# Three places for split weights instead of two, one of them in the fourth weight room, and the experts' gather copies shared out anew

## The chip, the cores and the metric

One core of one Trainium2 chip runs the whole program. The time is device microseconds of that core. TensorE (PE) multiplies, VectorE (DVE) and ScalarE (ACT) work on what lies in on-chip memory, GpSimd (POOL) does a little, and SyncE (SP) issues nearly all DMA transfers, in the order of its program.

## The reference

A sequence of 256 tokens, 2048 features, goes through two networks, all in float32:

- A first block: RMS norm, a projection to 5120 features (`w_in`), causal pooling and an HGRN2 recurrence, a projection back (`w_out`); cross attention to 256 memory rows (`wk`, `wq`, `wv`, `wo`, each 2048 x 2048); then a hierarchical mixture of experts with 16 experts of 512 features, each token going to 2 of them in one group of 4; then a norm.
- A second block, two layers: `mod = silu(c) @ w_ada + b_ada` (2048 x 6144 for each layer) gives shift, scale and gate; a norm with them, a projection to 6656 features (`w_in_2`, stages z0 and z1 here), four mixers (a 2-D Fourier transform with the matrix `w_fft`, neighbourhood attention, retention in both directions, a convolution of 31 taps with a pointwise matrix), and a projection back (`w_out_2`, stages mix0 and mix1).

## The kernel before

**Blocks.** All large weights come as blocks of 128 x 2048 float32, 1 MB each. The stages are w_in (40 blocks), w_out, wk, wq, wv, wo (16 each), the experts (192), z0 (52), mix0 (16), z1 (52), mix1 (16). Activations lie transposed, features on partitions, 256 tokens along the row.

**Split products.** A float32 product is made of three fp16 products. ScalarE scales a block by 256 and rounds it to fp16, the high half (`split` in its program, the instruction on L644). VectorE subtracts that from the scaled block, which gives the low half (L1292). TensorE then does high x high, low x high and high x low for each of 8 chunks and two halves of a block: 48 matmuls of 256 columns (`product`, L2241). Activations are split in the same way.

**Rooms and places.** A block passes two kinds of buffers. It lands in a room: `raw` has four, and the experts' stage has up to four more in memory that is free then (W, two in Y, one in Z). `raw_rooms` goes through all blocks in the order of loading and gives each the open room that was used longest ago. The small matrices pool_w, w_fft (`fft0`, `fft1`) and the pointwise one (`pw0`, `pw1`) take rooms too, without being split, and hold them until their own matmuls are done (L2818, L2839). From the room the halves are written to a place: `w_hi` and `w_lo` have two (SPL = 2), used in turn. In the experts' stage the same two places, taken together, are one half of a ring of four blocks, and W holds the other half.

**Who waits for whom.** SP loads a block when the room's last block has been split (`raw_taken`, counted by VectorE's low half, or by TensorE for a small matrix; L471). ScalarE splits a block when it has landed and when TensorE has finished the block that had the place (`block_done`). VectorE follows ScalarE (`hi_done`), and TensorE waits for VectorE (`raw_taken`). Each engine runs its program in order.

**The modulation.** The product with w_ada is done on VectorE, in 192 steps spread over the dense stages by a table (`ada_plan`): 16 loads of 512 KB for each of 12 parts, each followed by one multiply-add of 128 x 1024 into a running sum (`ada_step`, L1263, the first of a part L1260). They alternate between two buffers; a load waits until the step two before it has used its buffer (`ada_used`, L476). On VectorE the steps planned for block m come after the split of block m. On SP their loads come after the load of block m + 2 (`load_due(2)`), in the same queue. The table gives z0 and z1 thirteen steps over blocks 2 to 10 (two and one in turn) and one step a block from 11 to 29; wq and wv have 26 steps in 16 blocks, wo 20, mix0 16 over blocks 2 to 11, w_in 16 over 2 to 12, w_out 11, wk 13.

**The other work of VectorE** between splits in z0 and z1: four or so taps of the convolution after each block (L2008), the softmax parts of the attention, and in z0 the first network's last norm.

**The small matrices of z0 and z1.** w_fft is loaded behind block 43, and TensorE uses it just before block 45 (`fft_map`). The pointwise matrix is loaded behind block 48, and used just before block 47.

**The start of the experts.** The rows of the 256 tokens are gathered by group into 448 slots, in 16 chunks, by TensorE (L2556, a product with a matrix of zeros and ones, one for the high and one for the low halves). ScalarE copies the high part of each chunk out of its bank (L976, `gather_hi`), VectorE the low part (L1867, `gather_lo`). TensorE puts the gather of chunk b + 2 into block b and needs the copies of chunk b for block b; two chunks have banks at a time. VectorE has, between the same blocks, the second half of the rows' split (`rows_lo`) and the routing's small operations (`groups_left`, `best_two`, `combine`, `place_rows`).

The lines that matter in `raw_rooms` and in SP's program:

```
        open_ = list(range(RAW))
        if 0 <= j < n:
            open_ += [4] * (j >= 6) + [5] * (7 <= j < 126) + [6] * (j >= 7) + [7] * (13 <= j < 150)
        r = min(open_, key=lambda r: last[r])
```

```
                        load(ph, m, w[2 * n + j % 2, j // 2] if k == 0 and ph in K_MAJOR else w[2 * n + j // 2, j % 2])
                        due.append((ph, plan.get(ph, {}).get(m, [])))
                        load_due(2)
```

Of the kernel before, what the change touches and what calls it, by code (L numbers as in the profile page):

```python
# [8 lines left out]
F16 = mybir.dt.float16  # L9
# [14 lines left out]
ROOMS = RAW + 4  # L24
SPL = 2
IN_ORDER = [4, 5, 2, 3, 6, 7, 0, 1, 8, 9]
# [98 lines left out]
def raw_rooms():  # L125

    (first, _, n), total = places()["moe"], sum(n for _, n, _ in STREAM)
    rooms, uses, last = [], [0] * ROOMS, [-1] * ROOMS
    for b in range(total):
        j = b - first  # L130
        open_ = list(range(RAW))
        if 0 <= j < n:
            open_ += [4] * (j >= 6) + [5] * (7 <= j < 126) + [6] * (j >= 7) + [7] * (13 <= j < 150)
        r = min(open_, key=lambda r: last[r])
        uses[r], last[r] = uses[r] + 1, b
        rooms.append((r, uses[r]))
    return rooms
# [59 lines left out]
def build(nc, A, table, const_at, columns, router, out):  # L197
    ctx = ExitStack()
    with ctx:
# [20 lines left out]
        raw = sb("raw", [P, RAW, BLK])  # L220
        w_hi = sb("w_hi", [P, SPL, BLK], F16)
        w_lo = sb("w_lo", [P, SPL, BLK], F16)
        XT = sb("XT", [P, KC, T])
# [28 lines left out]
        y_hi, y_lo = (Zf[:, k * 1024:(k + 1) * 1024].bitcast(F16).rearrange("p (k n) -> p k n", n=512) for k in range(2))  # L252
        hid_at = [H[:, k * 1024:(k + 1) * 1024] for k in range(4)] + [Zf[:, c * T:c * T + 1024] for c in (28, 48)] + [Yf[:, k * 1024:(k + 1) * 1024] for k in range(2)]
        raw_at = [raw[:, r, :] for r in range(RAW)] + [w3, Yf[:, 0:BLK], Yf[:, BLK:2 * BLK], Zf[:, 40 * T:48 * T]]
        hid_t = [a[:, 0:2 * ROWS_SORTED].bitcast(F16).rearrange("p (c n) -> p c n", n=ROWS_SORTED) for a in hid_at]
# [41 lines left out]
        HI_AT = {"ga": 0, "pt": KC, "t": KC + 3, "y": KC + 3 + 4 * TILES}  # L297
        LO_AT = {"ga": 0, "weight": KC, "t": KC + 1, "y": KC + 1 + 4 * TILES}
        SQ_AT = {"x": 0, "wo": 4, "two": 12, "mix0": 18, "mix1": 26}
# [119 lines left out]

        def done(eng, ph, j, i=0):  # L420

            s = where(ph, j)[1]
            eng.wait_ge(block_done[s % SPL], s // SPL + 1 + 2 * i)

# [30 lines left out]
        def _(sp):  # L455
# [5 lines left out]
            def load(ph, j, src):  # L461
                r, n = rooms[where(ph, j)[0]]
                if n > 1:
                    sp.wait_ge(raw_taken[r], n - 1)
                elif r == 4:
                    sp.wait_ge(ada_mod, 7)
                elif r in (5, 6):
                    done(sp, "wo", 15)
                elif r == 7:
                    sp.wait_ge(S("rows_lo"), 10)  # L470
                sp.dma_start(raw_at[r], src).then_inc(raw_full[r], 16)  # L471
# [149 lines left out]
        def _(act):  # L621
            def split_half(ph, j, half):

                b, s = where(ph, j)
                r, n = rooms[b]
                if half == 0:
                    act.wait_ge(raw_full[r], 16 * n)
                    act.wait_ge(block_done[s % SPL], s // SPL)
                cut = slice(half * BLK // 2, half * BLK // 2 + BLK // 2)
                act.activation(w_hi[:, s % SPL, cut], raw_at[r][:, cut], ACT.Copy, scale=W_SCALE).then_inc(hi_done, 1)  # L630

            def split(ph, j, i=0):
                b, s = where(ph, j)
                r, n = rooms[b]
                act.wait_ge(raw_full[r], 16 * n)
                if ph == "moe":
                    act.wait_ge(block_done[s % SPL], s // SPL - 1)
                    if j < 2:
                        act.wait_ge(S("x_o"), 2 * X_HEADS)
                    w = ring_hi[j // 2 % 2][:, j % 2 * BLK:j % 2 * BLK + BLK]  # L640
                else:
                    act.wait_ge(block_done[s % SPL], s // SPL + 2 * i)
                    w = w_hi[:, s % SPL, :]
                act.activation(w, raw_at[r], ACT.Copy, scale=W_SCALE).then_inc(hi_done, 1)  # L644
                if (ph, j) in parts_due:
                    ada_high(parts_due[ph, j])
# [327 lines left out]
            def gather_hi(c):  # L974
                act.wait_ge(S("moe_mm"), MM_AT["ga"] + c + 1)
                act.activation(xs_hi[:, c, :], gather_bank(c, 0), ACT.Copy).then_inc(S("moe_hi"), 1)  # L976

# [35 lines left out]
            for n in range(MOE_STEPS):  # L1013
                f, last = n // 8, n % 8 == 7
                for part in range(2):
# [16 lines left out]
                    if n >= 17 and n % 16 == 1 and n < GATE_UP + 3:  # L1032
                        for k in (2 * part, 2 * part + 1):
                            turned_hi(n // 16 - 1, k)
                    if n == 2 and part == 1:
                        act.wait_ge(S("r_exp_in"), 1)
# [204 lines left out]
        def _(dve):  # L1241
# [34 lines left out]
            def split_half(ph, j, half):  # L1276

                b, s = where(ph, j)
                dve.wait_ge(hi_done, s + 1 + half)
                cut = slice(half * BLK // 2, half * BLK // 2 + BLK // 2)  # L1280
                ins = dve.scalar_tensor_tensor(w_lo[:, s % SPL, cut], raw_at[rooms[b][0]][:, cut], W_SCALE, w_hi[:, s % SPL, cut], ALU.mult, ALU.subtract)
                if half:
                    ins.then_inc(raw_taken[rooms[b][0]], 1)

            def split(ph, j, i=0):
                b, s = where(ph, j)
                dve.wait_ge(hi_done, s + 1 + 4 * i + (s > at["z1"][1]))
                hi, lo = w_hi[:, s % SPL, :], w_lo[:, s % SPL, :]
                if ph == "moe":
# [575 lines left out]
            def gather_lo(c):  # L1865
                dve.wait_ge(S("moe_mm"), MM_AT["ga"] + c + 1)
                dve.tensor_copy(xs_lo[:, c, :], gather_bank(c, 1)).then_inc(S("moe_lo"), 1)  # L1867

# [31 lines left out]
            for n in range(MOE_STEPS):  # L1900
                f, last = n // 8, n % 8 == 7
                for part in range(2):
# [23 lines left out]
                    if part == 1:  # L1926
                        if n == 0:
                            groups_left()
                        if n == 2:
                            best_two()  # L1930
                        if n == 5:
                            combine()
                        if n in (3, 4):
                            place_rows(n - 3)
                    if n == 6 and part == 1:
# [285 lines left out]
        def _(pe):  # L2221
            def product(ph, j, b, k0, start, stop, groups=None, x=(xh, xl), rows=False, between=None):

                s = at[ph][1] + j
                hi = w_hi[:, s % SPL, :].rearrange("p (c n) -> p c n", c=8)
                lo = w_lo[:, s % SPL, :].rearrange("p (c n) -> p c n", c=8)
                first = start
# [316 lines left out]
            def gather(c):  # L2544
                if c >= 2:
                    pe.wait_ge(S("moe_hi"), HI_AT["ga"] + c - 1)
                    pe.wait_ge(S("moe_lo"), LO_AT["ga"] + c - 1)
                if c == 2:
# [10 lines left out]
            def turn_places():  # L2559
                pe.wait_ge(S("moe_hi"), HI_AT["ga"] + KC)  # L2560
                pe.wait_ge(S("moe_lo"), LO_AT["ga"] + KC)
                pe.wait_ge(S("placed"), 4)
# [80 lines left out]
            for n in range(MOE_STEPS):  # L2643
# [8 lines left out]
                for c in range(2):  # L2652
                    taken(pe, "moe", 2 * n + c)
                    if f == 0:
                        pe.wait_ge(S("moe_hi"), HI_AT["ga"] + 2 * n + c + 1)
                        pe.wait_ge(S("moe_lo"), LO_AT["ga"] + 2 * n + c + 1)
                    if f == 8 and kh % 2 == 0 and c == 0:
# [336 lines left out]
```

## Time and profile before

| | |
|---|---|
| median of 3 runs | 2095.44 us (2094.69 to 2101.43) |
| the profiled execution's own time | 2093.71 us |
| its span | 2091.7 us |
| granted TensorE clock, mean | 0.994 |
| TensorE matmul busy | 2041.4 us (98%) |
| VectorE busy | 1752.3 us (84%) |
| ScalarE busy | 1194.1 us (57%) |
| DMA, mean over the span | 284 GB/s |

The profiled execution's time holds 2 us beside the span, from the first to the last instruction. "Busy" of TensorE is the union of its matmuls, whose ends are modelled: they start every 0.11 us and are shown 0.27 us long, so a gap in the rows is some 0.16 us shorter than what was lost. In the rows, PE, DVE and ACT are TensorE, VectorE and ScalarE, and SPq is SyncE's queue of DMA issues. L1292 is line 1292 of the kernel. A row such as `w_lo<-raw,w_hi` gives output and inputs by their names in the program. `[0.63 <-DVE w_lo L1292]` says that the engine stood idle for 0.63 us before the instruction, and what ended that.

### The profile page before, as it was taken

To read this page: it belongs to the slowest core of one execution; us is meant where nothing else is said; L and a number is where in the kernel's file an instruction comes from. 1 tells how busy PE (TensorE), PEld (TensorE's weight loads), DVE (VectorE), ACT (ScalarE), POOL (GpSimd) and SP (SyncE) were. 2 spreads that over 40 slices of the span, in tenths; PEclk is the share of its full clock that TensorE was granted. 3 is DMA by queue.
4 is the path that set the end of the run, shared out by engine and by line. 5 is a ranking of instruction groups with operands and counts; after the bars stand their busy time and mean duration, and the time that the engine had idled before them with its cause. 6 is when DMAs were issued, how large, how long until landed. Compare 5 with 4: busy or idle time off the path is not lost.

```text
span 2091.7 us, 42599 instructions
## 1 busy us (share of the span) xinstructions
PE 2041.4 (98%) x18993; PEld 1641.1 (78%) x18993; DVE 1752.3 (84%) x1670; ACT 1194.1 (57%) x1071; POOL 41.3 (2%) x40
## 2 busy tenths in 40 slices
PE   8999999999999989999999999999999899999998
PEld 7889888888889946555556568888888788888887
DVE  7875787988888799999999999999668779996555
ACT  5554644444445478877877864456554444565543
POOL 0002300000000000000000000000000000000000
PEclk9999999999999999999999999999999999999999
DMA  8854487789888878999999987874458778744452
GB/s 303 317 202 162 163 314 271 280 307 326 319 326 298 309 280 355 420 420 420 420 420 416 408 318 293 294 256 164 143 184 310 281 286 304 250 162 159 181 202 101
DMA packets 95717, 593.23 MB, mean 284 GB/s; under 512 B 10664, under 2 KB 10824, under 8 KB 36784
## 3 DMA queue, kind: packets, MB, share of 16 engines
q1 hardware_dynamic: 94912, 583.73, 74.4%
q0 software_dynamic: 624, 6.80, 0.8%
q8 instruction: 149, 2.44, 0.5%
q14 instruction: 32, 0.26, 0.0%
HBM read 588.39 MB, written 2.10 MB: 282 GB/s over the span
## 4 chain that ended last, share of the span: by engine, by line
PE 68%; DVE 16%; DMA 10%; ACT 3%; issue 3%; DVEq 0%; SPq 0%; POOL 0%; ACTq 0%; POOLq 0%
PE GB L2241 52%; DVE w_lo L1292 6%; PE GB L2670 4%; DVE W L1292 3%; PE MB L2670 3%; DMA raw<-w_up 3%; DMA W<-w_ada 2%; ACT w_hi L644 2%; DMA Z<-w_ada 2%; DMA raw<-w_down 2%; DVE W L1263 1%; DVE Z L1263 1%; DMA raw<-w_gate 1%; PE MB L2839 1%; PE MB L2441 1%
## 5 line engine op out<-in xcount | busy, mean ns | idle before, releaser
L644 ACT ACTIVATE w_hi<-raw 128x2048 f16<-128x2048 f32 x308 | 588.1, 1910 | 705.5 <-PE GB L2241 680.9
L1292 DVE SCALAR_TENSOR_TENSOR w_lo<-raw,w_hi 128x2048 f16<-128x2048 f32 x308 | 706.0, 2294 | 244.9 <-ACT w_hi L644 244.2
L2241 PE MATMUL GB<-H,w_hi 128*128 128x256 f16 x4352 | 718.9, 273 | 18.3 <-DVE w_lo L1292 11.6
L2241 PE MATMUL GB<-H,w_lo 128*128 128x256 f16 x2176 | 593.8, 273 | 0.0
L2241 PEld LDWEIGHTS GB<-H,w_hi 128*128 128x128 f16 x4352 | 421.6, 98 | 85.0 <-DVE w_lo L1292 16.6
L2241 PEld LDWEIGHTS GB<-H,w_lo 128*128 128x128 f16 x2176 | 213.2, 98 | 24.9
L2241 PE MATMUL GB<-w_hi,H 128*128 128x256 f16 x1280 | 210.7, 273 | 0.0
L1263 DVE SCALAR_TENSOR_TENSOR W<-W,SM 128x1024 f32<-128x1024 f32 x120 | 153.8, 1282 | 31.8 <-DMA W<-w_ada 28.5
L2241 PE MATMUL GB<-w_lo,H 128*128 128x256 f16 x640 | 174.4, 273 | 0.0
L2241 PE MATMUL GB<-Z,w_hi 128*128 128x256 f16 x1024 | 170.0, 274 | 2.9 <-DVE w_lo L1292 2.9
L2241 PE MATMUL GB<-W,w_hi 128*128 128x256 f16 x1024 | 168.0, 273 | 2.7 <-DVE w_lo L1292 2.7
L2241 PE MATMUL GB<-Z,w_lo 128*128 128x256 f16 x512 | 140.4, 274 | 0.0
L2241 PE MATMUL GB<-W,w_lo 128*128 128x256 f16 x512 | 139.6, 273 | 0.0
L2241 PEld LDWEIGHTS GB<-w_hi,H 128*128 128x128 f16 x1280 | 124.7, 98 | 16.1 <-issue 1.3
L1292 DVE SCALAR_TENSOR_TENSOR W<-raw,W 128x2048 f16<-128x2048 f32 x54 | 123.2, 2286 | 2.3 <-ACT W L644 2.2
L644 ACT ACTIVATE W<-raw 128x2048 f16<-128x2048 f32 x54 | 103.0, 1911 | 20.9 <-DMA raw<-w_down 6.1
L2241 PEld LDWEIGHTS GB<-Z,w_hi 128*128 128x128 f16 x1024 | 100.4, 98 | 16.0 <-DVE w_lo L1292 3.8
L2241 PEld LDWEIGHTS GB<-W,w_hi 128*128 128x128 f16 x1024 | 99.9, 98 | 14.9 <-DVE w_lo L1292 3.3
L2008 DVE SCALAR_TENSOR_TENSOR Y<-Y,PC 128x256 f32<-128x256 f32 x240 | 99.6, 479 | 0.0
L2670 PE MATMUL GB<-W,Z 128*64 (+1 forms) x864 | 86.7, 353 | 4.4 <-DVE Z L1867 4.3
L2670 PE MATMUL MB<-W,Z 128*64 (+1 forms) x864 | 86.0, 353 | 1.3 <-DVE W L1292 1.2
L1263 DVE SCALAR_TENSOR_TENSOR Z<-Z,SM 128x1024 f32<-128x1024 f32 x60 | 76.8, 1281 | 10.7 <-DMA Z<-w_ada 9.9
(489 smaller groups left out, 2789.9 us busy)
## 6 DMA issues: line engine op xcount, KB each, us to landing
raw<-w_in SPq DMA_DIRECT2D x144, 1024.0 KB, 5.2
W<-w_ada SPq DMA_DIRECT2D x128, 512.0 KB, 5.6
raw<-w_out SPq DMA_DIRECT2D x48, 1024.0 KB, 5.1
raw<-w_down SPq DMA_DIRECT2D x41, 1024.0 KB, 10.6
raw<-w_gate SPq DMA_DIRECT2D x34, 1024.0 KB, 11.0
raw<-w_up SPq DMA_DIRECT2D x32, 1024.0 KB, 12.8
Z<-w_ada SPq DMA_DIRECT2D x64, 512.0 KB, 5.9
raw<-xattn_wk SPq DMA_DIRECT2D x16, 1024.0 KB, 5.1
```

The source lines that it names most:

```text
L644: act.activation(w, raw_at[r], ACT.Copy, scale=W_SCALE).then_inc(hi_done, 1)
L1263: dve.scalar_tensor_tensor(sums, w, SM[:, 24 + k:25 + k], sums, ALU.mult, ALU.add).then_inc(ada_used[n % 2], 1)
L1292: dve.scalar_tensor_tensor(lo, raw_at[r], W_SCALE, hi, ALU.mult, ALU.subtract).then_inc(raw_taken[r], 1)
L2008: dve.scalar_tensor_tensor(ca[:, c, :], CU[:, c, k // 4:k // 4 + T], col("conv_w_2", l * TAPS * 4 + k), ca[:, c, :], ALU.mult, ALU.add).th ...
L2241: last = pe.matmul(o, a, m, start=first, stop=end and w_part is lo, skip_group_check=True)
L2441: ins = pe.matmul(MB[:, h % 2, a * T:a * T + T], x_q[q][:, 4 * h + c, a * P:a * P + P], x_k[k][:, 4 * h + c, :], start=a == 0 and c == 0 a ...
L2670: ins = pe.matmul(o_bank(j, k)[r:r + SLOT], x[:, c0 + c, at_:at_ + SLOT], v, start=kh == 0 and c == 0 and part == 0, stop=kh == 7 and c == ...
L2839: ins = pe.matmul(banks[:, n // 2, n % 2 * T:n % 2 * T + T], w[:, k, n * P:n * P + P], x[:, k, :], start=n % 2 == 0 and k == 0, stop=k == ...
```

## The change

- SPL is 3. The third place for split weights lies in the fourth room (`raw[:, 3]`, which holds both halves of one block). `slot` turns a block's number into its place. The dense stages use three rooms and three places; the experts' stage has the fourth room back from its fifth block on.
- The first load into that room in the experts' stage waits for block 13 of wo, the last that was split there. The first block of z0 waits until the room is given up.
- In the gather, ScalarE copies both parts of odd chunks, first the low and then the high one; VectorE copies the low part of even chunks alone. LO_AT and the waits of TensorE count accordingly.
- groups_left comes two steps later, best_two one step, the second place_rows two, the first one step; ScalarE's first exponential comes one step later.

```diff
-SPL = 2
+SPL = 3
...
-        open_ = list(range(RAW))
+        open_ = list(range(RAW - 1))
         if 0 <= j < n:
-            open_ += [4] * (j >= 6) + [5] * (7 <= j < 126) + [6] * (j >= 7) + [7] * (13 <= j < 150)
+            open_ += [3] * (j >= 4) + [4] * (j >= 6) + [5] * (7 <= j < 126) + [6] * (j >= 7) + [7] * (13 <= j < 150)
...
+        third = raw[:, RAW - 1, :].bitcast(F16)
+        hi_of = [w_hi[:, 0, :], w_hi[:, 1, :], third[:, 0:BLK]]
+        lo_of = [w_lo[:, 0, :], w_lo[:, 1, :], third[:, BLK:2 * BLK]]
+
+        def slot(s):
+
+            return (s + 2) % SPL
...
                 if n > 1:
                     sp.wait_ge(raw_taken[r], n - 1)
+                elif r == RAW - 1:
+                    done(sp, "wo", 13)
...
                 if ph == "moe":
-                    act.wait_ge(block_done[s % SPL], s // SPL - 1)
+                    act.wait_ge(block_done[(s - 4) % SPL], (s - 4) // SPL + 1)
...
                 else:
-                    act.wait_ge(block_done[s % SPL], s // SPL + 2 * i)
-                    w = w_hi[:, s % SPL, :]
+                    act.wait_ge(block_done[s % SPL], s // SPL)
+                    if (ph, j) == ("z0", 0):
+                        given_up(act, RAW - 1)
+                    w = hi_of[slot(s)]
...
             def gather_hi(c):
                 act.wait_ge(S("moe_mm"), MM_AT["ga"] + c + 1)
+                if c % 2:
+                    act.activation(xs_lo[:, c, :], gather_bank(c, 1), ACT.Copy)
                 act.activation(xs_hi[:, c, :], gather_bank(c, 0), ACT.Copy).then_inc(S("moe_hi"), 1)
...
             def gather_lo(c):
-                dve.wait_ge(S("moe_mm"), MM_AT["ga"] + c + 1)
-                dve.tensor_copy(xs_lo[:, c, :], gather_bank(c, 1)).then_inc(S("moe_lo"), 1)
+                if c % 2 == 0:
+                    dve.wait_ge(S("moe_mm"), MM_AT["ga"] + c + 1)
+                    dve.tensor_copy(xs_lo[:, c, :], gather_bank(c, 1)).then_inc(S("moe_lo"), 1)
...
-                        if n == 0:
+                        if n == 2:
                             groups_left()
-                        if n == 2:
+                        if n == 3:
                             best_two()
                         if n == 5:
                             combine()
-                        if n in (3, 4):
-                            place_rows(n - 3)
+                        if n in (4, 6):
+                            place_rows(n // 2 - 2)
...
-                    pe.wait_ge(S("moe_lo"), LO_AT["ga"] + c - 1)
+                    pe.wait_ge(S("moe_lo"), LO_AT["ga"] + c // 2)
...
-                        pe.wait_ge(S("moe_lo"), LO_AT["ga"] + 2 * n + c + 1)
+                        pe.wait_ge(S("moe_lo"), LO_AT["ga"] + n + 1)
```

## Rows read from the trace of the kernel before

**Rows 1.** Waits of TensorE and VectorE: us in total, times, longest
```profile
PE GB L2241 <- DVE w_lo L1292: 17.3, 20, 2.1
PE GB L2670 <- DVE Z L1867: 5.2, 5, 1.6
...
DVE W L1263 <- DMA W<-w_ada: 28.5, 33, 1.8
DVE Z L1263 <- DMA Z<-w_ada: 9.9, 9, 2.7
```
**Rows 2.** The page's groups: busy us, mean ns | idle before them, releaser
```profile
L644 ACT ACTIVATE w_hi<-raw 128x2048 f16<-128x2048 f32 x308 | 588.1, 1910 | 705.5 <-PE GB L2241 680.9
```
**Rows 3.** Timeline of TensorE in wk and mix0: start us, us, instruction, idle before
```profile
402.03 0.39 PE L2241 MATMUL GB<-H,w_hi 128*128 128x256 f16 x2 [0.63 <-DVE w_lo L1292]
...
1633.61 0.39 PE L2241 MATMUL GB<-W,w_hi 128*128 128x256 f16 x2 [1.49 <-DVE w_lo L1292]
```
**Rows 4.** Timeline of SP's queue in z0: start us, us of the issue
```profile
1321.11 0.33 SPq L471 DMA_DIRECT2D raw<-w_in  x1
1322.31 0.33 SPq L476 DMA_DIRECT2D Z<-w_ada  x1
```
**Rows 5.** Timeline of VectorE in z0, the same stretch
```profile
1318.79 2.29 DVE L1292 SCALAR_TENSOR_TENSOR w_lo<-raw,w_hi 128x2048 f16<-128x2048 f32 x1
1320.99 1.28 DVE L1263 SCALAR_TENSOR_TENSOR Z<-Z,SM 128x1024 f32<-128x1024 f32 x1
1322.19 1.67 DVE L2008 SCALAR_TENSOR_TENSOR Y<-Y,PC 128x256 f32<-128x256 f32 x4
1323.77 2.29 DVE L1292 SCALAR_TENSOR_TENSOR w_lo<-raw,w_hi 128x2048 f16<-128x2048 f32 x1
```
**Rows 6.** w_ada issued behind weights: two from 300.5, two from 331.9, three from 402.4
```profile
DMA to landing us min/median/max: 5.9/6.4/6.8
...
DMA to landing us min/median/max: 5.7/6.5/7.3
...
DMA to landing us min/median/max: 7.0/8.3/8.5
```
**Rows 7.** Windows: span, busy PE, PEld, DVE, ACT, POOL, clock, DMA share, GB/s
```profile
1267.00:1316.00 49.00, 47.51 (x432) 42.11 (x432) 45.97 (x49) 20.52 (x15) 0.00 (x0) 1.00 0.92 350
1316.00:1360.00 44.00, 43.84 (x412) 38.90 (x413) 43.09 (x55) 19.20 (x14) 0.00 (x0) 1.00 0.84 294
1360.00:1440.00 80.00, 79.43 (x707) 66.82 (x705) 79.52 (x115) 49.51 (x82) 0.00 (x0) 1.00 0.64 221
738.00:775.00 37.00, 33.27 (x280) 15.76 (x282) 34.97 (x46) 28.93 (x29) 0.00 (x0) 1.00 0.79 286
```
**Rows 8.** Chain of waits in wq, from one head's scores to the next's
```profile
496.87 2.62 PE MB L2441 x24
499.49 15.72 PE GB L2241 x144
...
520.89 2.62 PE MB L2441 x24
```
**Rows 9.** SP's wait for w_fft's room, that load's landing, the chain behind
```profile
SPq L471 <- PE GB L2818: 22.9, 1, 22.9
...
DMA to landing us min/median/max: 4.8/4.8/4.8
...
1528.96 10.64 PE GB L2241 x96
1539.60 6.92 PE MB L2839 x32
```
**Rows 10.** A wait of TensorE at the experts' start, and the gather's copies
```profile
754.00 0.84 PE L2670 MATMUL GB<-W,Z 128*64 x6 [1.65 <-DVE Z L1867]
...
L1867 DVE CAST Z<-MB x16: 616/618/625, 735.8 to 789.9; 128x448 f16<-128x448 f32 x16
...
L976 ACT ACTIVATE Z<-MB x16: 521/526/543, 735.8 to 786.9; 128x448 f16<-128x448 f32 x16
```

More of the change, by code:

```diff
@@ L220, in build @@
         raw = sb("raw", [P, RAW, BLK])
-        w_hi = sb("w_hi", [P, SPL, BLK], F16)
-        w_lo = sb("w_lo", [P, SPL, BLK], F16)
+        w_hi = sb("w_hi", [P, 2, BLK], F16)
+        w_lo = sb("w_lo", [P, 2, BLK], F16)
         XT = sb("XT", [P, KC, T])
@@ L297, in build @@
         HI_AT = {"ga": 0, "pt": KC, "t": KC + 3, "y": KC + 3 + 4 * TILES}
-        LO_AT = {"ga": 0, "weight": KC, "t": KC + 1, "y": KC + 1 + 4 * TILES}
+        LO_AT = {"ga": 0, "weight": KC // 2, "t": KC // 2 + 1, "y": KC // 2 + 1 + 4 * TILES}
         SQ_AT = {"x": 0, "wo": 4, "two": 12, "mix0": 18, "mix1": 26}
@@ L418, in piece_end, with done @@
             return 2 + u if i == 0 and ph in K_MAJOR else 4 * i + 2 * u + 1
-        def done(eng, ph, j, i=0):
+        def done(eng, ph, j):
             s = where(ph, j)[1]
-            eng.wait_ge(block_done[s % SPL], s // SPL + 1 + 2 * i)
+            eng.wait_ge(block_done[s % SPL], s // SPL + 1)
         def pieces_in(eng, k):
@@ L629, in split_half @@
                 cut = slice(half * BLK // 2, half * BLK // 2 + BLK // 2)
-                act.activation(w_hi[:, s % SPL, cut], raw_at[r][:, cut], ACT.Copy, scale=W_SCALE).then_inc(hi_done, 1)
+                act.activation(hi_of[slot(s)][:, cut], raw_at[r][:, cut], ACT.Copy, scale=W_SCALE).then_inc(hi_done, 1)
             def split(ph, j, i=0):
@@ L1034, in _ @@
                             turned_hi(n // 16 - 1, k)
-                    if n == 2 and part == 1:
+                    if n == 3 and part == 1:
                         act.wait_ge(S("r_exp_in"), 1)
@@ L1280, in split_half @@
                 cut = slice(half * BLK // 2, half * BLK // 2 + BLK // 2)
-                ins = dve.scalar_tensor_tensor(w_lo[:, s % SPL, cut], raw_at[rooms[b][0]][:, cut], W_SCALE, w_hi[:, s % SPL, cut], ALU.mult, ALU.subtract)
+                ins = dve.scalar_tensor_tensor(lo_of[slot(s)][:, cut], raw_at[rooms[b][0]][:, cut], W_SCALE, hi_of[slot(s)][:, cut], ALU.mult, ALU.subtract)
                 if half:
@@ L1287, in split @@
                 dve.wait_ge(hi_done, s + 1 + 4 * i + (s > at["z1"][1]))
-                hi, lo = w_hi[:, s % SPL, :], w_lo[:, s % SPL, :]
+                hi, lo = hi_of[slot(s)], lo_of[slot(s)]
                 if ph == "moe":
@@ L2224, in product @@
                 s = at[ph][1] + j
-                hi = w_hi[:, s % SPL, :].rearrange("p (c n) -> p c n", c=8)
-                lo = w_lo[:, s % SPL, :].rearrange("p (c n) -> p c n", c=8)
+                hi = hi_of[slot(s)].rearrange("p (c n) -> p c n", c=8)
+                lo = lo_of[slot(s)].rearrange("p (c n) -> p c n", c=8)
                 first = start
@@ L2560, in turn_places @@
                 pe.wait_ge(S("moe_hi"), HI_AT["ga"] + KC)
-                pe.wait_ge(S("moe_lo"), LO_AT["ga"] + KC)
+                pe.wait_ge(S("moe_lo"), LO_AT["ga"] + KC // 2)
                 pe.wait_ge(S("placed"), 4)
```

## The prediction, made before the change was run

> **What bounds the kernel now.** Read the busy table first: TensorE is busy 98% of the span, so at most the rest can come back, and any stall put into it counts in full. Then TensorE's waits [rows 1]: 20 waits in the dense stages for the low half of a weight block (17.3 us), and 5 for VectorE's gather copies (5.2 us). VectorE in turn waits for w_ada, 38 us in 42 waits, in the same group. Third, the split itself [rows 2]: ScalarE makes the high half in 1.91 us and idles 681 us waiting for TensorE to give a place back. With two places the split of a block can't begin before the block two ahead is done; a block is 5.24 us of TensorE (three take 15.72, [rows 8]), and 1.91 + 2.29 us of split leave about 1 us for delays. That is what produces the 20 waits; two are shown [rows 3].
>
> Last, who feeds VectorE. SP's queue is in order: weight load, then the modulation loads (w_ada, 512 KB) of the block two earlier, then the next weight load. A weight load waits for a free room, i.e. for VectorE's split of the block that had it. In [rows 4, 5] the split at 1318.79 ends at 1321.08 and the load goes out at 1321.11; the step at 1320.99 ends at 1322.27 and the next w_ada load goes out at 1322.31. That load is used two blocks on. VectorE's block there is 4.98 us (1318.79 to 1323.77): split 2.20, step 1.20, four taps 1.58 (start to start, as everywhere below), with no DMA wait.
>
> **The rooms.** With three rooms instead of four, the load of block m+2 waits for the split of m-1, not of m-2, and w_ada for block m comes behind it in SP's queue. So w_ada for m cannot be issued before the split of m-1 has ended, plus 0.10 us and the 0.37 us of the weight load's issue, and VectorE wants it about 5 us after that same moment. How long such a load takes, directly behind a weight block, is in [rows 6]: seven of them, 5.7 to 8.5 us. I take 6.4 (the median of the first two groups, whose queue is otherwise empty, as it would be); 5.7 and 7.3 are my ends. The cover that hid it was the second block of distance; it is gone.
>
> This makes a loop of two blocks on VectorE that TensorE has no part in, so that a third place for split weights can't shorten it: end of split m-1, 0.47, landing 6.4, steps of m, work behind them, split of m+1 (2.20).
> - Middle of z0 and z1 (blocks 11 to 19, one step, taps 1.58): 0.47 + 6.4 + 1.20 + 1.58 + 2.20 = 11.85, 5.93 us a block. TensorE needs 5.4 ([rows 7]: 43.8 us busy, eight blocks and their small work). 9 x 0.53 = 4.8 us.
> - Blocks 3 to 10 (every other one has two steps): 0.47 + 6.4 + 2.40 + 2.20 = 11.5, 5.75 us; now 49 us for nine, 5.44 [rows 7]. 8 x 0.31 = 2.5 us.
> - Blocks 20 to 29: VectorE is full there (79.5 of 80 us, [rows 7]; some 6.5 us a block, 3.1 of it behind the step): 0.47 + 6.4 + 1.2 + 3.1 + 2.2 = 13.4, 6.7 us. 10 x 0.2 = 2 us.
>
> That is 9.3 us in each of z0 and z1, 18.6 in all. At 5.7 us it is 1.6 each (3 in all), at 7.3 it is 21 each (42).
>
> The Trainium skill (DMA: Bandwidth & Descriptors, "Anatomy of one DMA") gives a DMA a fixed 2.0 us and its bytes at 436 GB/s, in a fit for the gpsimd path. By it the 1.5 MB of a weight block and a w_ada load behind it would be down 5.6 us after the first issue, so 5.2 after the second. The trace does not agree: its fastest is 5.7 and its median over 6 [rows 6]. By the page the middle blocks would take 5.33 us, and the loop would cost nothing.
>
> The same loop elsewhere:
> - w_in, blocks 2 to 12: 1.5 steps a block, little behind them; 5.65 against 5.24, less idle time that VectorE has at its start: +3 (0 to +7).
> - w_out, wk: steps are sparse and VectorE has slack ahead of the waits, so a place in advance takes up what delays there are: -1.5 (two waits such as [rows 3]'s first, with some 0.16 us of pipeline each). The longest wait of [rows 1], 2.1 us at w_out's start, is one for the order of ScalarE's work and stays. The room of pool_w now goes to w_out's second block; its release at 260.1 still leaves several us before that split. Ends -4 and +3.
> - wq, wv, wo: four blocks take 24.0 us [rows 8], 6.0 each. A two-step block makes the loop 0.47 + 6.4 + 2.4 + 0.9 + 2.2 = 12.4, 6.2 a block; with the one-step blocks between, 6.1 to 6.3. Over 48 blocks 5 to 14 us, of which one place in advance absorbs 5: +4 (0 to +15).
> - mix0: VectorE enters it idle, so the place in advance is full and covers 5.24 us of a lag of about 6.4, where TensorE now waits some 2.7 in all (its last in [rows 3]): -1.5 (-3 to +3).
>
> **The small matrices in z0 and z1.** The w_fft matrix takes a room from its load until its matmuls at block 45. With four rooms the next in that room is block 47; with three it is block 46. SP's wait for it is in [rows 9] (22.9 us, off the path today). After: the load goes out at 1528.8, lands 4.8 us later (1533.6), high half 1.91 + 0.05, low half 2.29: ready at 1537.9. TensorE starts block 45 at 1528.96 and is through it at 1534.2. +3.7 us in each of z0 and z1, +7.4; no split place helps, since the raw data is not there. The pointwise matrix now waits for the split of block 46 (1537.9) and lands about 5 us later, when TensorE is through with that block (1543.1): it adds 0 to 2. Ends +7 and +12 for both.
>
> **The experts' rows.** VectorE drops eight copies of 0.62 us (0.54 apart), ScalarE gains eight of 0.53 (0.45 apart), [rows 10]. VectorE is the full one (35.0 of 37 us against 28.9, the last of [rows 7]). Walked from 741: chunk 3's copy, now behind ScalarE's split of block 4, is ready near 746.8 where block 3 wants it at 748.0: that wait goes. ScalarE's extra copy of chunk 1 delays splits 2 and 3 by 0.45. For block 4 VectorE loses chunk 3's copy (0.54) and groups_left (1.12, moved to step 2), and the copy ends at 752.7 instead of 753.86: the 1.65 wait becomes about 0.5 plus what block 3 starts earlier. Blocks 5 to 8 then start on time, in place of waits of 0.61 and 0.51. Block 8 starts at 765.9 instead of 768.5: -2.6 us. best_two, combine and place_rows only change place (same instructions). The weight loads follow VectorE's splits, so they move with it and the DMA-bound part behind keeps the gain. Ends: -4 (all waits gone) and +1 (ScalarE late, or DMA takes it back).
>
> The waits on the last room before and after the experts (block 13 of wo; the room given up at block 187) are met long before; the first block loads of the experts need one room more to be split, some 25 us ahead of use: 0.
>
> **Sum.** 18.6 + 3 - 1.5 + 4 - 1.5 + 7.4 - 2.6 = +27.4. On the profiled execution's own time, 2093.71 us: 2121. The median of the three runs lies 1.7 above that execution; I keep 2121.
>
> **Rivals.**
> - *The lead wins (faster).* If w_ada behind a weight block lands under 5.35 us (2 x 5.4 less 0.47, 1.20, 1.58 and 2.20), the loop costs nothing; the 14 waits that aren't ones of a stage's start (six, 6.4 us) go (17.3 - 6.4 = 10.9, plus 14 x 0.16), and the experts' 2.6: -15.7; with the w_fft room +7.4, -8.3: 2085, or 2078 if that is covered too. For: VectorE idles hundreds of us behind ScalarE, so slack exists. Against: not in the stretches with steps, where it idles under 1 us per 40. Chance 0.10. The page's reckoning above (the Trainium skill, "Anatomy of one DMA") would put it here.
> - *It cancels (no change).* Landings at the low end (5.7): +3 for z, +1 for w_in, +7.4, and -11 from w_out to wk, mix0 and the experts at their low ends: 2094, 2098 if one of them gives less. Chance 0.08.
> - *The pair of loads is slow (much slower).* With 7.3 us or more, as in [rows 6]'s last group, and in the first part of z0 where the DMA engines are 92% busy [rows 7]: 42 for z, 6 for w_in, 14 for wq to wo, 9 for the small matrices: about 2160. Chance 0.16.
> - *The forecast*: 0.66.
>
> This kernel's measurement tells about 0.3% (6 us) from no change. Faster 0.10, same 0.08, slower 0.82. The likeliest case's own range is 2104 to 2140; for 8 in 10 I take 2094 to 2146, which leaves out most of the faster case and the slow end.
>
> **What would show it.** VectorE's waits for w_ada grow from 38 us to over 80, most in z0 and z1, blocks 4 to 19; SP's weight and w_ada issues stand 0.4 us apart there; TensorE's waits for the low half grow at regular 5.9 us steps. One TensorE wait of 3 to 5 us at block 46 in z0 and z1. The waits for L1867 fall from 5.2 to under 3 us. ScalarE's wait for TensorE falls where no steps are (mix1). It is wrong if w_ada behind a weight block lands under 5.3 us, or if TensorE's waits total less than now.

## The result, and the profile after

The changed kernel takes 2161.61 us (median of 4 runs, 2157.32 to 2178.05) against 2095.07 us: ratio 1.0325, 95% interval 1.0265 to 1.0385. It is slower, as forecast, by 66.5 us where 27.4 were forecast (+25.9 against the 2095.07 median); the time lies above the range (2094 to 2146). The profiled execution is the slowest of the four, 2178.05 us with a span of 2176.2, so its terms add up to 84.5 us, not to 66.5. A trace nearer to the median comes from an experiment below.

The totals first: the page of the changed kernel, its span and TensorE's row, and the first lines of its chain of waits.

```profile
span 2176.2 us, 42599 instructions
...
PE 2069.2 (95%) x18993; PEld 1646.7 (76%) x18993; DVE 1750.2 (80%) x1662; ACT 1197.4 (55%) x1079; POOL 42.5 (2%) x40
...
PE 28%; DMA 23%; issue 23%; DVE 23%; ACT 3%; SPq 1%; POOLq 0%; DVEq 0%; POOL 0%; ACTq 0%
PE GB L2256 17%; DMA W<-w_ada 14%; DVE w_lo L1306 8%; DVE W L1277 4%; PE GB L2685 3%; DVE W L1306 3%; PE MB L2685 3%; DMA Z<-w_ada 3%; DMA raw<-w_up 3%; DVE raw L1306 2%; DMA raw<-w_down 2%; ACT w_hi L656 2%; DMA raw<-w_gate 1%; DVE Z L1277 1%; PE MB L2571 1%
```

The span grew by 84.5 us. TensorE has the same 18993 matmuls, but was busy 27.8 us longer (2041.4 to 2069.2); the other 56.7 us are idle time. Those are two different costs, and the prediction had only the second. Of the 27.8 us, 22.2 are a lower clock (below); much of the rest is waits that the rows show too short, by 0.16 us for each of the 39 waits for low halves that are new (an estimate: 6 us). The waits (us in total, times, longest), which answer to [rows 1]:

```profile
DVE W L1277 <- DMA W<-w_ada: 117.7, 69, 4.6
PE GB L2256 <- DVE w_lo L1306: 52.2, 40, 3.9
DVE Z L1277 <- DMA Z<-w_ada: 39.3, 30, 3.5
PE GB L2256 <- DVE raw L1306: 21.8, 19, 3.6
DVE W L1274 <- DMA W<-w_ada: 9.0, 2, 5.5
```

VectorE's waits for w_ada went from 38 us to 157 for L1277 alone (41 to 166 with the first steps of a part, L1274); TensorE's waits for a low half from 17.3 to 74.0 us (59 times; "raw" is the third place, in the fourth room). The difference, 56.7 us, is as large as the growth of TensorE's idle time.

**The loop, in z1.** Timeline of SP's queue, then of VectorE, in the changed kernel (start us, us, instruction, idle before it):

```profile
1804.85 0.33 SPq L481 DMA_DIRECT2D raw<-w_in  x1
1805.22 0.43 SPq L486 DMA_DIRECT2D Z<-w_ada  x1
```

```profile
1802.54 2.28 DVE L1306 SCALAR_TENSOR_TENSOR w_lo<-raw,w_hi 128x2048 f16<-128x2048 f32 x1
...
1809.03 2.28 DVE L1306 SCALAR_TENSOR_TENSOR raw<-raw 128x2048 f16<-128x2048 f32 x1
1813.37 1.28 DVE L1277 SCALAR_TENSOR_TENSOR Z<-Z,SM 128x1024 f32<-128x1024 f32 x1 [2.06 <-DMA Z<-w_ada]
1814.57 1.67 DVE L2023 SCALAR_TENSOR_TENSOR Y<-Y,PC 128x256 f32<-128x256 f32 x4
1816.16 2.29 DVE L1306 SCALAR_TENSOR_TENSOR w_lo<-raw,w_hi 128x2048 f16<-128x2048 f32 x1
```

The split at 1802.54 ends at 1804.82, the weight load goes out at 1804.85, w_ada at 1805.22, and the step that needs it starts at 1813.37, behind the next block's split: 8.15 us after the issue. From split to split over two blocks that is 13.62 us, 6.8 a block, with the terms of the forecast and a landing of 8.15 in place of 6.4. Landings over a whole stretch: w_ada in z1, 1740 to 1830, and in wq to wo, 475 to 740.

```profile
DMA to landing us min/median/max: 3.5/5.9/8.1
...
DMA to landing us min/median/max: 3.6/5.8/8.6
```

The median is below the 6.4 that I took; the longest is above my slow end. These windows hold every w_ada load. The loads of the loop, those issued within half a microsecond behind a weight load, are 90 in the whole trace, and took 5.6 us at least, 5.9 in the median, 6.4 in the mean and 10.4 at most.

**The clock.** Behind a TensorE wait of 2.16 us (it ends at 1785.99), windows of one microsecond: span, busy PE, PEld, DVE, ACT, POOL, granted clock, DMA share, GB/s.

```profile
1785.00:1786.00 1.00, 0.01 (x1) 0.01 (x1) 0.93 (x1) 1.00 (x1) 0.00 (x0) 1.00 0.30 119
1786.00:1787.00 1.00, 1.00 (x6) 0.74 (x7) 0.23 (x1) 0.91 (x1) 0.00 (x0) 0.57 0.45 66
1787.00:1788.00 1.00, 1.00 (x7) 0.69 (x6) 1.00 (x2) 0.00 (x0) 0.00 (x0) 0.50 0.68 147
1788.00:1789.00 1.00, 1.00 (x6) 0.75 (x5) 1.00 (x2) 0.00 (x0) 0.00 (x0) 0.50 0.89 377
1789.00:1790.00 1.00, 1.00 (x9) 0.78 (x7) 1.00 (x1) 0.00 (x0) 0.00 (x0) 0.73 1.02 422
1790.00:1791.00 1.00, 1.00 (x12) 0.89 (x10) 0.26 (x1) 0.00 (x0) 0.00 (x0) 1.00 0.96 393
```

The matmul counts show it too: 6 or 7 a microsecond instead of 12. The granted clock is at its lower level, 1.2 GHz, for some 3.4 us, and (0.43 + 0.50 + 0.50 + 0.27) = 1.7 us of work is lost on top of the wait. Over the whole span the mean clock is 0.984 against 0.994. Lost clock is span times what the mean lacks: 34.8 us against 12.6. The profiled execution had more of it than most: over all executions the changed kernel lost 30 us (4 of them), the kernel before 16 (26 of them, beside the first experiments). So of the 66 us some 14 are clock, and the rest is not.

**Block 46 of z0.** Timeline of TensorE in the changed kernel, and windows from the DFT's matmuls to the pointwise ones, which took 15.9 us before (the chain in [rows 9] has it without a wait):

```profile
1589.02 0.61 PE L2256 MATMUL GB<-H,w_hi 128*128 128x256 f16 x2 [3.91 <-DVE w_lo L1306]
```

```profile
1574.30:1597.10 22.80, 18.74 (x131) 15.06 (x131) 4.99 (x3) 12.29 (x10) 0.00 (x0) 0.85 0.50 185
1589.00:1596.00 7.00, 6.99 (x38) 5.14 (x39) 1.60 (x2) 6.94 (x8) 0.00 (x0) 0.57 0.44 150
```

The wait is 3.9 us, as worked out (3.7); behind it the clock is low for six of seven microseconds, 3 us more.

### The profile page after: what moved, and what is told of

Read it like the earlier page. It is cut to its first block, busy times and chain, and to the rows that moved or that the text cites. A ratio compares the mean times of both kernels' runs of the same rounds, so it can differ in the third digit from the quotient of the medians.

```text
span 2176.2 us, 42599 instructions
## 1 busy us (share of the span) xinstructions
PE 2069.2 (95%) x18993; PEld 1646.7 (76%) x18993; DVE 1750.2 (80%) x1662; ACT 1197.4 (55%) x1079; POOL 42.5 (2%) x40
## 4 chain that ended last, share of the span: by engine, by line
PE 28%; DMA 23%; issue 23%; DVE 23%; ACT 3%; SPq 1%; POOLq 0%; DVEq 0%; POOL 0%; ACTq 0%
PE GB L2256 17%; DMA W<-w_ada 14%; DVE w_lo L1306 8%; DVE W L1277 4%; PE GB L2685 3%; DVE W L1306 3%; PE MB L2685 3%; DMA Z<-w_ada 3%; DMA raw<-w_up 3%; DVE raw L1306 2%; DMA raw<-w_down 2%; ACT w_hi L656 2%; DMA raw<-w_gate 1%; DVE Z L1277 1%; PE MB L2571 1%
## 5 line engine op out<-in xcount | busy, mean ns | idle before, releaser
L1306 DVE SCALAR_TENSOR_TENSOR w_lo<-raw,w_hi 128x2048 f16<-128x2048 f32 x223 | 511.1, 2295 | 106.8 <-ACT w_hi L656 106.4
L656 ACT ACTIVATE w_hi<-raw 128x2048 f16<-128x2048 f32 x223 | 424.8, 1905 | 194.7 <-PE GB L2256 114.0
L2256 PE MATMUL GB<-H,w_hi 128*128 128x256 f16 x2880 | 482.5, 275 | 31.8 <-DVE w_lo L1306 29.4
L2256 PE MATMUL GB<-H,w_lo 128*128 128x256 f16 x1440 | 395.4, 275 | 0.0
L2256 PEld LDWEIGHTS GB<-H,w_hi 128*128 128x128 f16 x2880 | 280.1, 99 | 80.1 <-DVE w_lo L1306 37.4
L2256 PE MATMUL GB<-H,raw 128*128 128x256 f16 x2208 | 254.4, 276 | 17.9 <-DVE raw L1306 14.3
L2256 PEld LDWEIGHTS GB<-H,raw 128*128 128x128 f16 x2208 | 215.9, 99 | 54.1 <-DVE raw L1306 18.7
L1277 DVE SCALAR_TENSOR_TENSOR W<-W,SM 128x1024 f32<-128x1024 f32 x120 | 154.0, 1283 | 121.4 <-DMA W<-w_ada 117.7
L1306 DVE SCALAR_TENSOR_TENSOR raw<-raw 128x2048 f16<-128x2048 f32 x85 | 195.3, 2298 | 40.3 <-ACT raw L656 39.9
L656 ACT ACTIVATE raw<-raw 128x2048 f16<-128x2048 f32 x85 | 161.9, 1904 | 94.9 <-PE GB L2256 52.1
L2256 PEld LDWEIGHTS GB<-H,w_lo 128*128 128x128 f16 x1440 | 142.0, 99 | 17.3
L2256 PE MATMUL GB<-Z,w_hi 128*128 128x256 f16 x672 | 114.3, 277 | 11.5 <-DVE w_lo L1306 11.4
L1277 DVE SCALAR_TENSOR_TENSOR Z<-Z,SM 128x1024 f32<-128x1024 f32 x60 | 76.9, 1282 | 40.2 <-DMA Z<-w_ada 39.3
```

The source lines that it names most:

```text
L1277: dve.scalar_tensor_tensor(sums, w, SM[:, 24 + k:25 + k], sums, ALU.mult, ALU.add).then_inc(ada_used[n % 2], 1)
L1306: dve.scalar_tensor_tensor(lo, raw_at[r], W_SCALE, hi, ALU.mult, ALU.subtract).then_inc(raw_taken[r], 1)
L2256: last = pe.matmul(o, a, m, start=first, stop=end and w_part is lo, skip_group_check=True)
```

## The experiments

Times are medians beside the kernel before on the same chip; in brackets the 95% interval of the ratio.

**rooms3: the room alone.** The kernel before, with

```
-        open_ = list(range(RAW))
+        open_ = list(range(RAW - 1))
-            open_ += [4] * (j >= 6) + ...
+            open_ += [3] * (j >= 4) + [4] * (j >= 6) + ...
```

> The kernel before with three raw rooms instead of four in the dense stages; two places for split weights as before, the experts' copies as before. Theory (the loop over w_ada: SP issues the w_ada loads of a block only after the split of the block just ahead, and VectorE waits for them; TensorE's longer waits then lower its clock): nearly the whole loss is here, 2150 to 2180 us, VectorE's waits for w_ada over 120 us, mean clock 0.985 or less. Rival (the third place itself, its order on ScalarE or the shared room, makes the loss): 2095 to 2110 us.

2168.26 us against 2095.3, 1.0341 (1.0322 to 1.0360). The loss is whole without the third place: 73.0 us against 66.5, with intervals that overlap. Its waits:

```profile
DVE W L1263 <- DMA W<-w_ada: 99.2, 67, 3.4
PE GB L2241 <- DVE w_lo L1292: 70.6, 61, 4.1
DVE Z L1263 <- DMA Z<-w_ada: 35.4, 33, 3.0
```

The rival is out. The mean clock came out at 0.988, not at 0.985 or less.

**near: the order of w_ada in SP's queue.** The changed kernel, with

```
-                        load_due(2)
+                        load_due(1)
```

> The whole change, but SP issues the w_ada loads of a block directly after the weight load of the next block (one block behind instead of two), so they no longer stand behind the load that waits for the split of the block just ahead. Theory: the loop is open again, w_ada waits fall under 60 us; what is left is the w_fft room, 3.9 us of stall and about 3 us of lower clock in z0 and in z1 (14 us), less some 10 us of waits that the third place takes up: 2097 us, 2088 to 2108. Rival (three rooms are too few for the weight loads themselves, whoever is ahead of them in the queue): above 2140 us, with ScalarE's waits for raw as long as now.

2095.56 us against 2095.3, 1.0003 (0.9993 to 1.0014): one line in SP's queue takes 66 us away, three rooms and all. Its waits:

```profile
DVE W L1277 <- DMA W<-w_ada: 40.1, 48, 2.5
DVE Z L1277 <- DMA Z<-w_ada: 11.6, 13, 2.1
PE GB L2256 <- DVE w_lo L1306: 10.6, 8, 3.9
PE GB L2256 <- DVE raw L1306: 7.8, 6, 3.4
```

Three rooms carry the weight loads well; no_third and near4_gather, below, differ in the fourth room. What they don't carry is a w_ada load that stands behind a weight load waiting for the split just ahead. The two long TensorE waits left are at block 46 of z0 and z1 (the first, and the windows of the same piece as above):

```profile
1534.32 0.61 PE L2256 MATMUL GB<-H,w_hi 128*128 128x256 f16 x2 [3.92 <-DVE w_lo L1306]
...
1519.60:1542.20 22.60, 18.53 (x131) 14.99 (x131) 4.78 (x3) 12.08 (x10) 0.00 (x0) 0.85 0.50 186
```

**near_fft44: another room for w_fft.** As near, and

```
-FFT_AFTER, PW_AFTER = 43, 48
+FFT_AFTER, PW_AFTER = 44, 48
```

> As near, and w_fft is loaded one block later (after block 44), which moves it to another room: block 46 then takes the room of block 44, and the room of w_fft goes to block 47. Theory: TensorE's wait of 3.9 us at block 46 goes in z0 and z1, and the low clock behind it: 12 to 14 us less than near, about 2083 us. Rival (the wait has another cause, such as w_fft's late landing in front of block 45's matmuls): within 3 us of near.

2086.63 us, 0.9962 (0.9943 to 0.9981); 8.9 us less than near. In its trace no TensorE wait is left there, and the piece is back at its old length:

```profile
1521.20:1537.00 15.80, 15.65 (x131) 13.64 (x131) 4.89 (x4) 9.87 (x9) 0.00 (x0) 1.00 0.55 205
```

Between the two traces the piece is 6.8 us shorter in z0 and 4.7 in z1, 11.5 in all, of which 8.9 show in the medians; I had expected 12 to 14 in time.

**after_fft44: the same edit alone**, in the changed kernel.

> The changed kernel with nothing but w_fft loaded one block later, which moves it to another room. Theory: the waits of 3.9 and 3.6 us at block 46 and the low clock behind them go, as they did in the pair near and near_fft44 (9 us there): 2148 to 2154 us against 2162. Rival (VectorE is so late there that the next load sets the same pace): within 3 us of 2162.

2155.13 us against 2097.46, 1.0270 (1.0233 to 1.0307). Against the 66.5 us of the changed kernel it loses 57.7: 8.8 us less (6.5 by the plain medians, just outside the band expected). The two intervals overlap, so that the edit works here is shown by the trace (the table below has the blocks 45 and 46 at their old length), not by the times. Its trace (span 2156.6) serves as the one nearer to the median in the table below.

**stall_short and stall_long: the price of a TensorE wait.** The kernel before; ScalarE, in mix1:

```
+                if ph == "mix1" and j in (4, 7, 10, 13):
+                    for _ in range(1):        # 2 in stall_long
+                        act.activation(w, raw_at[r], ACT.Copy, scale=W_SCALE).then_inc(S("again"), 1)
+                        again[0] += 1
+                        act.wait_ge(S("again"), again[0])
                 act.activation(w, raw_at[r], ACT.Copy, scale=W_SCALE).then_inc(hi_done, 1)
```

> The kernel before; in the last stage (mix1), where nothing but TensorE's 5.24 us a block sets the pace, ScalarE makes the high half twice in blocks 4, 7, 10 and 13. The second time adds 1.9 to 2.0 us, of which about 1 us is slack: four TensorE waits of about 1.0 us. Both theories (a wait costs its length; a longer wait also lowers TensorE's clock): +4 us, 2099 us, no stretch of lower clock in mix1.

> The same, with the high half made three times in those four blocks: four TensorE waits of about 2.9 us, 11.7 us in all. If the clock falls to half behind each such wait, as the trace of the changed kernel shows behind waits of 2.2 to 3.9 us, each costs some 1.7 us more: +18 us, 2113 us, and four stretches of about 3.4 us at half the clock. Rival (a wait costs its length and no more; the low clock is a coincidence of the crowded stages): +12 us, 2107 us, clock 1.00 through mix1.

2101.84 and 2114.82 us against 2097.46: +4.4 (1.0018, 1.0002 to 1.0035) and +17.4 (1.0075, 1.0050 to 1.0100). TensorE's timelines, one of the four waits of stall_short, then the first two and the third of stall_long:

```profile
2022.80 0.39 PE L2248 MATMUL GB<-W,w_hi 128*128 128x256 f16 x2 [1.09 <-DVE w_lo L1299]
```

```profile
2023.50 0.39 PE L2248 MATMUL GB<-W,w_hi 128*128 128x256 f16 x2 [3.03 <-DVE w_lo L1299]
2042.42 0.41 PE L2248 MATMUL GB<-W,w_hi 128*128 128x256 f16 x2 [3.03 <-DVE w_lo L1299]
2063.02 0.52 PE L2248 MATMUL GB<-W,w_hi 128*128 128x256 f16 x2 [3.03 <-DVE w_lo L1299]
```

Windows behind those three waits, in stall_long:

```profile
2023.50:2029.00 5.50, 5.50 (x51) 4.94 (x52) 3.08 (x3) 0.87 (x1) 0.00 (x0) 1.00 0.78 238
2042.00:2048.00 6.00, 5.58 (x36) 4.37 (x37) 3.95 (x5) 1.54 (x3) 0.00 (x0) 0.72 0.75 244
2063.00:2069.00 6.00, 5.98 (x40) 4.66 (x41) 3.64 (x4) 0.89 (x1) 0.00 (x0) 0.72 0.79 255
```

All four waits are 3.03 us (the fourth ends at 2083.61), and behind three of them the clock fell, behind the first not. The distance between the first two is 18.92 us, between the next two 20.60: the low clock costs 1.68 us. 4 x 3.03 + 3 x 1.68 = 17.2, measured 17.4. The five executions agree: in the mean they lost 4.8 us more clock than the kernel before, three falls' worth, and 12.2 us more beside it. Behind the waits of 1.09 us it stayed at 1.00. I had expected four falls; there were three.

The Trainium skill ("TensorE: Matmul & The Clock Gate", "HAM oscillation — how this bites in real kernels") describes a kernel in which waits for DMA between groups of matmuls bring the clock down again and again, so that the penalty is paid many times. The traces here agree in kind, with 1.68 us lost at three of the four waits and nothing at the first.

**gather_only and near4_gather: the experts' part alone,** with four rooms and two places; the second with `load_due(1)` as well.

> The kernel before with the experts' part alone: ScalarE copies both parts of the odd chunks, the routing steps are moved; four raw rooms, two places. As predicted: 2.6 us faster, 2092.5 us. Rival, from the trace of the changed kernel, where the gain of 1.7 us by block 10 of the experts is given back at block 28: no change, 2095 us within 1.

> Four raw rooms and two places for split weights, as before, with the experts' part of the change and the w_ada loads issued one block behind. If the nearer w_ada loads are worth something by themselves: VectorE's w_ada waits fall from 38 to 25 us or less and the time to about 2088 us. Rival (w_ada isn't late with four rooms, and loads issued earlier only stand in SP's queue ahead of the weights): 2093 us, as gather_only.

gather_only: 2093.07 us against 2095.3, 0.9988 (0.9975 to 1.0000); near4_gather: 2091.71 against 2097.46, 0.9968 (0.9954 to 0.9983). The experts' part gives 2.2 us by the medians, at the edge of what can be told from nothing. The nearer w_ada loads would be worth some 4 us by the two ratios (0.9968 against 0.9988), but the intervals overlap, and the sign expected did not come: VectorE's waits for w_ada are 32.3 us, against 33.7 in gather_only, not 25 or less. With four rooms a gain from them is not shown. In gather_only the five waits of [rows 1] on the gather's copies (one is in [rows 10]) are one, the second row here:

```profile
PE MB L2567 <- DVE Z L1840: 2.5, 1, 2.5
PE GB L2681 <- DVE Z L1878: 2.4, 1, 2.4
```

The first is ahead of the gather (VectorE's table of places); near that point the trace of before shows no such row, so I don't count it either way.

**no_third and near_fft44_again: the price of the third place.** near_fft44 with `SPL = 2`, on one chip with near_fft44 itself.

> near_fft44 without the third place: three raw rooms in the dense stages, two places for split weights, the experts' part of the change, w_ada one block behind, w_fft after block 44. It prices the third place where the w_ada loop is open. Theory (one place in advance takes up what delays there are, as the first rows of TensorE's waits said): TensorE's waits for the low half are 10 us or more longer than in near_fft44 (14.4 us), the time 8 to 12 us longer, 2095 to 2099 us. Rival (the third place is worth nothing; the order of the w_ada loads made all the difference): 2086 to 2089 us.

> near_fft44 once more, beside no_third on the same chip: ratio to the kernel before 0.994 to 0.998 as the first time, 2083 to 2090 us.

no_third: 2092.76 us against 2097.33, 0.9977 (0.9962 to 0.9992). near_fft44 again: 2086.80, 0.9941 (0.9921 to 0.9961), so its gain over the kernel before is there on both chips. no_third has three rooms and two places and takes as long as near4_gather with four and two (2092.76 and 2091.71 us, 0.9977 and 0.9968 with intervals that overlap): with the w_ada loads one block behind, the fourth room is worth nothing that these runs can tell. The third place is worth 6.0 us where the w_ada loop is open, less than the 8 to 12 expected. TensorE's waits, no_third first, then near_fft44_again:

```profile
PE GB L2252 <- DVE w_lo L1302: 17.6, 20, 2.1
```

```profile
PE GB L2256 <- DVE w_lo L1306: 10.5, 9, 4.0
PE GB L2256 <- DVE raw L1306: 4.9, 6, 1.9
```

That is 17.6 us against 15.4 (14.4 in the first trace of near_fft44), so waits for low halves account for 2 to 3 of the 6 us. The trace of near_fft44_again can't show the 6 us as it stands: its execution (2094.61 us) was slower than that of no_third (2093.01), with 22 us of lost clock against 12.6 and a wait of 4.0 us in w_in that the first trace has not. Without the clock, w_out and wk together are 3.5 us shorter than in no_third in both traces of near_fft44. Over all executions, what is not clock is 7 to 9 us less with the third place, near the 8 to 12 expected, and 2 to 3 us more of lost clock go against it. Which waits beside those for low halves make it up stays open.

## Why the prediction was wrong, step by step

Growth of each stretch in us, between the same instructions of TensorE (first matmuls of the norms, of the attention's scores, of the gather, the DFT and the pointwise product) in each trace and in the one of before:

| stretch of before, us | forecast | changed kernel (span 2176.2) | of it, lost clock | after_fft44 (2156.6) | rooms3 (2168.4) |
|---|---|---|---|---|---|
| 0 to 472: w_in, w_out, wk, start of wq | +1.5 | +20.4 | +1.7 | +18.5 | +20.1 |
| to 735: wq, wv, wo | +4 | +14.4 | -1.3 | +15.0 | +18.6 |
| to 1233: experts | -2.6 | +1.9 | +4.7 | +1.5 | +1.1 |
| to 1524: z0 to the DFT | +9.3 | +14.0 | +5.1 | +13.9 | +12.9 |
| to 1539: blocks 45 and 46 of z0 | +3.7 | +7.0 | +3.4 | 0 | +5.1 |
| to 1661: last blocks of z0, mix0 | -1.5 | +6.2 | +1.7 | +4.0 | +4.0 |
| to 1944: z1 to the DFT | +9.3 | +14.2 | +1.7 | +11.3 | +10.2 |
| to 1961: blocks 45 and 46 of z1 | +3.7 | +5.9 | +3.4 | +0.1 | +4.8 |
| to the end: mix1 | 0 | +0.5 | +1.5 | 0 | 0 |

"Lost clock" is the time in the stretch multiplied by what the granted clock lacks there, less the same in the trace of before. (One low stretch of before lies across 735, the border of the second and third row.)

**The mechanism was right.** The issues stand 0.37 us apart behind each split, w_ada's waits passed the 80 us that I named, and near removes nearly the whole loss by moving nothing but those issues. Block 46 was right in place and length. The final time went past the range because sizes were wrong, all to one side.

**Failed first: "the same loop elsewhere".** I gave w_in to wo and mix0 together +4 us (3 - 1.5 + 4 - 1.5); they took 41.0 in the profiled execution, 37.5 in after_fft44's, and only 2.1 of the 41.0 are clock. This is the largest error. The first stretch alone took 20.4: w_in, where 3 was forecast, has 8.6 of them (6.2 in after_fft44, 5.9 in rooms3), and w_out with wk, where -1.5 was forecast, 11.8 (12.3, 14.2). VectorE was held to have slack there; its waits for w_ada in w_out and wk were 39.5 us, against 9.3 before, so the loop was at work in them too. Three more parts can be read:
- I took the low value where the loop itself gave more: 5 to 14 us for wq to wo, and +4 was chosen. rooms3, with no third place, shows +18.6 there. The work behind the steps, 0.9 us in the sum, was right in the mean (0.96 a block from wq to wo), but it is unevenly spread. Here is VectorE in wq of the changed kernel, 4.6 us from a pair of steps to the next split:

```profile
527.99 2.68 DVE L1277 SCALAR_TENSOR_TENSOR W<-W,SM 128x1024 f32<-128x1024 f32 x2 [2.81 <-DMA W<-w_ada]
530.59 0.68 DVE L1680 SCALAR_TENSOR_TENSOR Z<-GB,Z 128x512 f16<-128x512 f32 x1
...
532.58 2.29 DVE L1306 SCALAR_TENSOR_TENSOR raw<-raw 128x2048 f16<-128x2048 f32 x1
```

  From 530.59 to 532.58 it is 2.0 us; behind the steps of the next three blocks it is 0.7, 0.6 and none. What the unevenness costs was not measured.
- The third place was to absorb about 5 us in wq to wo and to turn w_out, wk and mix0 into small gains. Against rooms3 it took up 3.6 to 4.2 us in wq to wo, at most 1.6 in the first stretch and none in mix0 and z. As I read it, a place in advance takes up a single delay, and where every block is late it is empty after the first.
- In w_out the w_ada load that is now due directly ahead of its step meets GpSimd's 2 MB load of mem. That load is issued at 284.1; the w_ada load of 286.44 takes 10.4 us where the one I counted with took 6.4, and VectorE waits 5.5 us for it, which TensorE sees as a wait of 3.0 us. The issue in SP's timeline, its landing, and VectorE:

```profile
286.44 0.43 SPq L486 DMA_DIRECT2D W<-w_ada  x1
...
DMA to landing us min/median/max: 10.4/10.4/10.4
```

```profile
296.87 0.75 DVE L1274 TENSOR_SCALAR W<-W,SM 128x1024 f32<-128x1024 f32 x1 [5.54 <-DMA W<-w_ada]
```

  The trace of before had such a load too: the one issued at 277.78, beside the same load of mem, took 11.2 us. VectorE did not wait for it, as the second block of distance covered it. It was there to be read, but [rows 6] begin only at 300.5.

**Failed second: the clock, which is in no term.** Lost clock grew by 22.2 us in the profiled execution, a quarter of the growth, and by some 14 in the mean of all executions, a fifth. I priced each wait at its length. [rows 3] already held waits of up to 1.5 us, and the clock's mean of 0.994 stood on the page; what a longer wait costs was not looked up in the trace, though w_out's wait of 2.05 us was in it, with the low clock behind it (0.66 over five microseconds). The same wait at the same place has none behind it in the changed kernel:

```profile
273.00:278.00 5.00, 5.00 (x31) 3.86 (x32) 5.00 (x4) 2.06 (x2) 0.61 (x1) 0.66 0.78 287
...
281.00:290.00 9.00, 8.46 (x78) 7.58 (x79) 8.86 (x9) 6.34 (x5) 0.61 (x1) 1.00 0.84 303
```

stall_long prices a fall at 1.7 us. In the small-matrix term it is the whole error in z0: 3.9 of wait as forecast (3.7) and 3.1 more (7.0); the wait in z1 was 3.6, the stretch 5.9.

**Third: one number for the landing. Its size held, in part by luck.** For the middle of z0 and z1 I forecast 9.3 each, with 6.4 us of landing; they took 14.0 and 14.2 (13.9 and 11.3 in after_fft44's trace). Part of that is the clock. Here are the stretches of z0 in which it was low, two of the changed kernel and the one of before; outside them it is 1.00:

```profile
1269.90:1300.00 30.10, 28.66 (x210) 25.26 (x209) 25.59 (x50) 16.97 (x29) 0.54 (x1) 0.83 0.51 197
1415.00:1430.00 15.00, 12.74 (x99) 10.19 (x98) 14.20 (x24) 9.26 (x18) 0.00 (x0) 0.89 0.71 261
...
1233.20:1260.00 26.80, 24.19 (x195) 21.09 (x194) 23.95 (x46) 16.20 (x26) 0.53 (x1) 0.94 0.55 218
```

That is 6.8 us of lost clock against 1.7, and 3.4 against 1.7 in z1. The 5.1 at z0's start are not of the loop: near, without it, loses 5.1 there too (1236 to 1247). Without the clock the growth is 8.9 and 12.5 (10.5 and 9.6 in after_fft44's trace), so 9.3 is near. With the median landing of 5.9 the forecast's own sum would give 3 us. The loads of the loop took 6.0 us in the mean in z0 and 6.4 in z1, and none was under the 5.35 at which the loop costs nothing, so each counts with its whole length: the mean belongs in the sum, not the median. That 6.4, a median of four loads, came near the mean of the 90 was luck. With the measured means the sum gives some 4 us for z0 and 9 for z1; what makes the rest, some 5 and 3 us, stays open.

**The rivals.** "The pair of loads is slow" gave 2160, the time that came, but not for its reason: it needed landings of 7.3 us or more, and the median is below 6. The page's reckoning (the Trainium skill, "DMA: Bandwidth & Descriptors", "Anatomy of one DMA"), 5.2 us and a loop that costs nothing, is further from the landings than my 6.4 was: no load of the loop was under 5.6, their median was 5.9, and the loop did cost. That is a fit for GpSimd's path, and these are loads of SP's queue. "The lead wins" and "it cancels" are out in this form; near is what the second would look like, near_fft44 the first.

**The experts.** -2.6 was forecast. Counted from 715 of before, the traces of the changed kernel, gather_only and near4_gather have gained 0.1 us or less at 770 and 0.2 at 825. Those of after_fft44, near, near_fft44 (both) and no_third have gained 2.4 to 2.8 at 770, as forecast, and keep 0.9 to 1.2 at 825: in all five the clock is low for 3.4 us in between (in near from 789), while gather_only has such a stretch at 754, behind its wait of 2.4 us. So in those five the steps gave what was worked out, and more than half of it was lost again where the clock is low. In its median gather_only is 2.2 us faster. That this part is worth something between 0 and 5 us is shown; how much reaches the end is not.

**A version that beats both.** near_fft44, the whole change with two constants set differently, 2086.6 to 2086.8 us, 0.4 to 0.6% under the kernel before.

## What to carry to other kernels

Before a buffer is taken away from one stream, look at what stands behind that stream's issues in the same queue: here the weight loads could spare the room, and the small loads queued behind them could not; a change of issue order was worth more than the buffer. Where a loop closes through a transfer, take the landings of loads issued as the loop will issue them, and their mean, not their median. Walk the loop through every stage that has the small loads, also where the engine seems to have slack. And price a TensorE wait from places in the trace where one of that length has happened, with the granted clock behind it; one place is not enough, as the clock does not fall every time.

## What the runs showed of the hardware

A TensorE wait of 3.03 us, forced four times in a stretch that was otherwise full, was followed three times by some 3.4 us at the lower clock (1.2 GHz), at 1.68 us apiece, and once by none. After 1.09 us, four times, it never was. In the changed kernel a wait of 3.91 us was followed by six microseconds of low clock out of seven, a wait of 2.16 us by 3.4.

Whether the clock falls behind a wait near 2 us is not settled by the wait. The same wait of 2.05 us stands at the start of w_out in all twelve traces. In six of them a low stretch follows (before, after_fft44, rooms3, near_fft44_again, no_third, near4_gather), in the other six none, and traces of one program differ in it (near_fft44 and near_fft44_again). Each fall is 1.7 us, so two executions of one kernel can differ by some microseconds from this alone.

Of 90 loads of 512 KB issued directly behind a 1 MB load in the changed kernel none landed in under 5.6 us; the median was 5.9, the mean 6.4. The longest, 10.4 us, ran beside a 2 MB load of another queue and a weight load; in the kernel before a load at that place took 11.2.
